# Latent attention: the rotary products of a head group moved ahead of its values, keys and queries, and the first group's opening written in another order

## The reference

```python
c_kv = rmsnorm(kv_a[..., :KV_LORA_RANK], ckv_norm)             # 128 wide, made earlier
k_nope = jnp.einsum('bsr,rhd->bshd', c_kv, w_uk)
v = jnp.einsum('bsr,rhd->bshd', c_kv, w_uv)
...
cq = rmsnorm(u @ w_dq, q_lora_norm)                            # 256 wide
q = jnp.einsum('bsr,rhd->bshd', cq, w_uq)
q_rope = apply_rope(q[..., QK_NOPE_DIM:], cos[None, :, None], sin[None, :, None])
...
s = (jnp.einsum('bqhd,bkhd->bhqk', qn_b, k_nope)
     + jnp.einsum('bqhr,bkr->bhqk', qr_b, k_rope))
p = jax.nn.softmax(s, axis=-1).astype(v.dtype)                 # causal, scaled
return jnp.einsum('bhqk,bkhd->bqhd', p, v)                     # 16 heads
```

## Time and profile before

| | |
|---|---|
| median of 3 runs | 1855.37 us (1854.82 to 1855.79) |
| the profiled execution | 1855.3 us, span of its instructions 1853.4 us |
| TensorE busy | 1823.8 us (98% of the span) |
| VectorE busy | 1568.9 us (85%) |
| ScalarE busy | 1148.2 us (62%) |
| GpSimd busy | 77.7 us (4%) |
| granted TensorE clock | 0.999 of full |

### The profile page before, as it was taken

How to read it: one execution, slowest core, us unless ns; L and a number is a source line. 1 busy time by engine, 2 the same in 40 slices (tenths; PEclk the granted TensorE clock), 3 DMA queues, 4 the chain that set the end, 5 groups by cost and what they waited for, 6 DMA issues and landing times.

```text
span 1853.4 us, 33830 instructions
## 1 busy us (share of the span) xinstructions
PE 1823.8 (98%) x13244; PEld 1702.7 (92%) x13244; DVE 1568.9 (85%) x1996; ACT 1148.2 (62%) x1478; POOL 77.7 (4%) x101
## 2 busy tenths in 40 slices
PE   8999999999999999999999999999999999999998
PEld 8999999999998889999999998899999998889997
DVE  7998899889886749997999799899889985879996
ACT  6665666666666637665666657666666656456664
POOL 1000100000000000000100000100010002010000
PEclk9999999999999999999999999999999999999999
DMA  7655465555553146555655443565545563345553
GB/s 273 216 196 200 164 217 196 190 182 204 204 196 144 48 149 215 205 204 182 216 204 198 145 146 117 194 242 203 202 169 207 199 214 122 119 149 183 207 195 107
DMA packets 61592, 339.18 MB, mean 183 GB/s; under 512 B 6976, under 2 KB 7360, under 8 KB 33088
## 3 DMA queue, kind: packets, MB, share of 16 engines
q1 hardware_dynamic: 59472, 330.00, 51.0%
q0 software_dynamic: 2032, 7.96, 1.2%
HBM read 336.89 MB, written 1.05 MB: 182 GB/s over the span
## 4 chain that ended last, share of the span: by engine, by line
PE 88%; DVE 7%; ACT 3%; issue 2%; DMA 1%; POOL 1%; DVEq 0%; SPq 0%; POOLq 0%; ACTq 0%
PE X L2051 60%; PE Y L2051 26%; DVE loA L1313 2%; DVE arena L1669 1%; DMA rawA<-in_wa 1%; ACT hiA L697 1%; DVE ol L1478 1%; PE X L2092 1%; ACT arena L1011 0%; DVE xs L1396 0%; DVE h L1403 0%; DVE arena L1834 0%; DVE arena L1771 0%; DVE xl L1353 0%; PE X L2075 0%
## 5 line engine op out<-in xcount | busy, mean ns | idle before, releaser
L2051 PE MATMUL X<-xh,hiA 128*128 128x256 f32 x2464 | 680.3, 278 | 6.0 <-DVE loA L1313 3.9
L2051 PE MATMUL X<-xl,hiA 128*128 128x256 f32 x2464 | 678.0, 277 | 0.0
L2051 PE MATMUL X<-xh,loA 128*128 128x256 f32 x2464 | 669.4, 277 | 0.0
L1313 DVE TENSOR_TENSOR loA<-rawA,hiA 128x2048 fp32r<-128x2048 f32 (+1 forms) x213 | 485.2, 2278 | 59.3 <-ACT hiA L697 59.0
L2051 PEld LDWEIGHTS X<-xh,hiA 128*128 128x128 f32 x2464 | 462.8, 188 | 8.9 <-DVE loA L1313 5.3
L2051 PEld LDWEIGHTS X<-xl,hiA 128*128 128x128 f32 x2464 | 463.4, 188 | 0.0
L2051 PEld LDWEIGHTS X<-xh,loA 128*128 128x128 f32 x2464 | 457.3, 188 | 0.0
L697 ACT ACTIVATE hiA<-rawA 128x2048 fp32r<-128x2048 f32 (+1 forms) x232 | 421.9, 1820 | 50.4 <-PE Y L2051 29.8
L852 ACT ACTIVATE act_sh<-X 128x512 f32<-128x512 f32 x168 | 100.7, 599 | 388.0 <-PE X L2051 388.0
L1524 DVE TENSOR_TENSOR sum_lo<-arena,sum_hi 128x2048 fp32r<-128x2048 f32 x72 | 164.5, 2285 | 1.5 <-ACT sum_hi L816 1.5
L816 ACT ACTIVATE sum_hi<-arena 128x2048 fp32r<-128x2048 f32 x72 | 137.2, 1905 | 0.0
(11 more groups left out here) (325 smaller groups left out, 3468.8 us busy)
## 6 DMA issues: line engine op xcount, KB each, us to landing
rawA<-in_wa SPq DMA_DIRECT2D x221, 1024.0 KB, 4.9
rawB<-in_wb SPq DMA_DIRECT2D x181, 512.0 KB, 4.1
row_gain<-in_rows POOLq DMA_DIRECT2D x8, 512.0 KB, 5.0
arena<-in_gla POOLq DMA_DIRECT2D x1, 1280.0 KB, 7.7
h<-in_x SPq DMA_DIRECT2D x2, 512.0 KB, 4.2
arena<-in_taps POOLq DMA_DIRECT2D x1, 576.0 KB, 4.9
arena<-in_pool POOLq DMA_DIRECT2D x1, 544.0 KB, 5.0
rawA<-in_wa SPq DMA_DIRECT2D x2, 256.0 KB, 6.4
```

Of the source, the lines that this page charges most:

```text
L1313: nc.vector.tensor_tensor(loA[p][:, cut], rawA[p][:, cut], hiA[p][:, cut].bitcast(f32), ALU.subtract).then_inc(a_lo, 1)
L2051: return say(nc.tensor.matmul(*args, **kw))
```

## The change

In groups 1 to 3 TensorE does the rotary products first, then the values, keys and queries. ScalarE copies each rotary bank into a new buffer `m_rope` in two extra copies per group, right behind the exponential of the same number, and that copy gives the bank back. VectorE turns from `m_rope` and tells so by a new semaphore `q_turned`, for which `scores` waits, and, for the buffer, the copy of two groups later. In group 0 the rotary products stay last and are turned out of the bank, but TensorE transposes the query latent before keys 0 and 1, starts the queries of heads 0 and 1 with the products of `cqh`, and does those of `cql` last; ScalarE copies the latent before `split_B(b + 1)` and does `split_A(a + 2)` behind the group's copies; VectorE puts `split_A(a + 2)` between the two turns and the second turn behind `maxima(0)`.

```diff
@@ -971,7 +973,7 @@
                 raw_squares(s, 1)
                 def values(g):
                     for t in range(TT):
-                        act.wait_ge(mproj_psum, 8 * g + 1 + t)
+                        act.wait_ge(mproj_psum, 8 * g + (3 if g else 1) + t)
                         nc.scalar.activation(m_v[:, g % 2, t, :], X[:, t, :], ACT.Copy
                                              ).then_inc(mproj_free[t], 1)
@@ -979,23 +981,28 @@
                     act.wait_ge(cq_psum, t + 1)
                     mean_square(s["norm_mid"] + t, Y[:, 2 + t, 0:2 * P], m_p[:, t, 0:2 * P], (2 * P) ** -0.5)
                 values(0)
-                split_B(b + 1, (b + 1) % 2)
                 for k in range(2):
                     act.wait_ge(cq_t, k + 1)
                     nc.scalar.activation(cqh[:, k, :], X[:, 2 + k, 0:TOKENS], ACT.Copy,
                                          scale=cols[:, COL["q_lora"] + k:COL["q_lora"] + k + 1]).then_inc(cq_hi, 1)
+                split_B(b + 1, (b + 1) % 2)
                 def projections(g, head=None):
                     n = a + 2 + g
                     if g:
+                        for p in range(2):
+                            exps(head, (p,))
+                            act.wait_ge(mproj_psum, 8 * g + 1 + p)
+                            if g > 1:
+                                act.wait_ge(q_turned, 2 * (g - 2) + p + 1)
+                            nc.scalar.activation(m_rope[:, p, :], X[:, p, 0:TOKENS], ACT.Copy
+                                                 ).then_inc(mproj_free[p], 1)
                         values(g)
                     for i in range(GROUP):
-                        if g and i < 2:
-                            exps(head, (i,))
                         if g == 1 and i >= 2:
                             split_A(n, n % 2, i - 2)
-                        act.wait_ge(mproj_psum, 8 * g + i + 3)
+                        act.wait_ge(mproj_psum, 8 * g + (5 if g else 3) + i)
                         nc.scalar.activation(m_qk[:, g % 2, i, :], X[:, i % 2 if g else i, :], ACT.Copy
                                              ).then_inc(mproj_free[i % 2], 1)
                     if g == 1:
...
@@ -1022,8 +1029,8 @@
                     act.wait_ge(mo_psum, i + 1)
                     nc.scalar.activation(oh(i), o_bank(i), ACT.Copy).then_inc(mo_hi, 1)
+                projections(0)
                 split_A(a + 2, a % 2)
-                projections(0)
                 for i in range(HEADS):
                     if i >= 2:
                         out_hi(i - 2)
...
@@ -1663,12 +1670,17 @@
             def turn_queries(g, p):
+                if g:
+                    dve.wait_ge(mproj_free[p], 4 * g + 1)
+                else:
+                    dve.wait_ge(mproj_psum, 7 + p)
                 for j in range(2):
                     rows = slice(64 * j, 64 * j + 64)
+                    straight = m_rope[rows, p, :] if g else X[rows, p, 0:TOKENS]
                     for part in range(2):
                         ins = nc.vector.tensor_tensor(m_qr[64 * part:64 * part + 64, g % 2, 2 * p + j, :],
-                                                      X[rows, p, 0:TOKENS], trig[rows, part, :], ALU.mult)
-                ins.then_inc(mproj_free[p], 1)
+                                                      straight, trig[rows, part, :], ALU.mult)
+                ins.then_inc(q_turned if g else mproj_free[p], 1)
             def latent(s):
                 norm_in(s)
...
@@ -1751,7 +1763,6 @@
                     elif g:
                         ahead(g)
                     for p in range(2):
-                        dve.wait_ge(mproj_psum, 8 * g + 7 + p)
                         turn_queries(g, p)
                 def maxima(i):
...
@@ -1776,10 +1787,13 @@
                     nc.vector.tensor_tensor(ol(i), o_bank(i), oh(i).bitcast(f32),
                                             ALU.subtract).then_inc(mo_lo, 1)
-                ahead(0)
-                projections(0)
+                split_B(b + 1, (b + 1) % 2)
+                turn_queries(0, 0)
+                split_A(a + 2, a % 2)
                 for i in range(HEADS):
                     maxima(i)
+                    if i == 0:
+                        turn_queries(0, 1)
                     if i >= 2:
                         out_lo(i - 2)
                     normalise(i)
...
@@ -2493,7 +2507,7 @@
                     m = b + g
                     pe.wait_ge(b_lo, m + 1)
                     for t in range(TT):
-                        bank(g, t)
+                        bank(g, 2 + t if g else t)
                         ins = by_tokens(X[:, t, :], ckvh[:, P * t:P * t + P], ckvl[:, P * t:P * t + P],
                                         hiB[m % 2][:, 512:1024], loB[m % 2][:, 512:1024], True, True)
                         ins.then_inc(mproj_psum, 1)
...
@@ -2533,8 +2547,6 @@
                 def projections(g):
                     n, m = a + 1 + g, b + g
-                    if g:
-                        values(g)
                     nh = hiA[n % 2][:, 0:1024].rearrange("p (h k c) -> p h k c", h=4, k=2)
                     nl = loA[n % 2][:, 0:1024].rearrange("p (h k c) -> p h k c", h=4, k=2)
                     rh = hiA[n % 2][:, 1024:1536].rearrange("p (h k c) -> p h k c", h=2, k=2)
...
@@ -2546,7 +2558,7 @@
                     def keys(i):
                         if g or i < 2:
-                            bank(g, 2 + i)
+                            bank(g, 4 + i if g else 2 + i)
                         by_latent(head_bank(i)[:, TOKENS:512], uh[:, P * i:P * i + P], ul[:, P * i:P * i + P],
                                   ckvh[:, :], ckvl[:, :], True, True)
...
@@ -2556,29 +2568,44 @@
                                             cql[:, k, :], k == 0, k == 1)
                         ins.then_inc(mproj_psum, 1)
+                    def rotary():
+
+                        wait_A(n)
+                        for p in range(2):
+                            bank(g, p if g else 6 + p)
+                            for k in range(2):
+                                ins = by_latent(X[:, p, 0:TOKENS], rh[:, p, k, :], rl[:, p, k, :], cqh[:, k, :],
+                                                cql[:, k, :], k == 0, k == 1)
+                            ins.then_inc(mproj_psum, 1)
+
                     if g == 0:
-                        for i in (2, 3, 0, 1):
-                            keys(i)
+                        keys(2)
+                        keys(3)
                         pe.wait_ge(cqs_done, 2)
                         query_latent()
-                        pe.wait_ge(cq_lo, 2)
+                        keys(0)
+                        keys(1)
                         pe.wait_ge(a_hi, n + 1)
                         pe.wait_ge(nope_lo, 1)
-                        for i in range(GROUP):
-                            queries(i)
+                        for k in range(2):
+                            pe.wait_ge(cq_hi, k + 1)
+                            for i in range(2):
+                                mm(X[:, i, 0:TOKENS], nh[:, i, k, :], cqh[:, k, :], start=k == 0, stop=False)
+                                mm(X[:, i, 0:TOKENS], nl[:, i, k, :], cqh[:, k, :], start=False, stop=False)
+                        pe.wait_ge(cq_lo, 2)
+                        for i in range(2):
+                            for k in range(2):
+                                ins = mm(X[:, i, 0:TOKENS], nh[:, i, k, :], cql[:, k, :], start=False, stop=k == 1)
+                            ins.then_inc(mproj_psum, 1)
+                        queries(2)
+                        queries(3)
+                        rotary()
                     else:
+                        rotary()
+                        values(g)
                         for i in range(GROUP):
                             keys(i)
-                            if i == 0:
-                                wait_A(n)
                             queries(i)
-                    wait_A(n)
-                    for p in range(2):
-                        bank(g, 6 + p)
-                        for k in range(2):
-                            ins = by_latent(X[:, p, 0:TOKENS], rh[:, p, k, :], rl[:, p, k, :], cqh[:, k, :], cql[:, k, :],
-                                            k == 0, k == 1)
-                        ins.then_inc(mproj_psum, 1)
                     owed.extend((a_free, b_free))
                 def scores(i):
...
@@ -2587,9 +2614,11 @@
                     if j == 0:
                         pe.wait_ge(mproj_free[0], 4 * g + 4)
                     if j == 1:
-                        pe.wait_ge(mproj_free[1], 4 * g + (2 if g else 3))
+                        pe.wait_ge(mproj_free[1], 4 * g + 3)
                     if j == 2:
                         pe.wait_ge(mproj_free[1], 4 * g + 4)
+                    if g and j % 2 == 0:
+                        pe.wait_ge(q_turned, 2 * (g - 1) + j // 2 + 1)
```

2 lines of the change are left out of this document (added).

## The result

The changed kernel takes 1858.23 us (median of 21 runs, 1857.0 to 1859.86) against 1855.29 us before (21 runs, 1854.62 to 1857.53): 2.94 us more. The ratio is 1.0016, with a 95% interval of 1.001 to 1.0022, so no change within 0.2%, though the interval lies above 1. The span of the profiled execution is 1856.9 us. ScalarE has six instructions more, the copies of the rotary banks (1484 in place of 1478), and TensorE as many matmuls as before.

The account below looks back on a forecast made before the run. TensorE is busy 98% of the span, so only its waits inside attention can change. Terms 2.17 - 0.59 - 0.33 = 1.25 us slower than the 1855.37 us median give 1856.6 us; range 1853.2 to 1859.3 us.

Parts of the forecast that it names:

- The upper end of the terms: Bounds of all terms together, -2.6 to +3.2 us; 3.2 lost if ScalarE's pieces in group 1 come 1 us later still.
- the low half's wait: Group 0: TensorE's wait of 1.26 us before the first query product, for the latent's low half, would be gone.
- new waits for the new copy: Groups 1, 2, 3: TensorE idle 1.4, 0.7 and 0.4 us before the first value product, released by the rotary copy.
- three signs of being wrong: Head 1's exponential well ahead of 591.4, ScalarE's second piece ending before 597.5, or a granted clock dip at 604 us.
- 2.17 us later than before: Group 1: `transpose_p(2)` at 606.57 in place of 604.40, VectorE's split and turns standing behind ScalarE's second piece.
- the opening: Group 0's new order: rotary products, first turn and scores of head 0 come 1.46 us earlier, between 1.2 and 1.53.
- Gain 0.59 us: Group 2: exponentials of head 6 start at 621.16 in place of 621.75 us.
- Gain 0.33 us: Group 3: `transpose_p(10)` comes at 641.33 in place of 641.66 us.
- the rival on the clock: Idle 2.8 us ahead of `transpose_p(2)` halves TensorE's clock: 1862.1 us, or 1859.3 if one head; chance 0.07.
- The turns' source: VectorE's turns from `m_rope` cost like turns from the bank; the skill's 0.065 us less each was not followed.
- The turns leave the path everywhere: Rival: all five TensorE waits shown in attention go, 5.75 us, 1849.6 us; chance 0.06.
- A part of it: Rival: group 1 even or keeps 0.80 us because ScalarE's pieces catch up, 1853.6 to 1854.4 us; chance 0.10.

Follow-up runs that it names:

- e3: Changed kernel with VectorE's two turns in group 1 put ahead of the split that waits for ScalarE: 1854.15 us, -0.46 against before.
- e4: Changed kernel with ScalarE's two pieces of the weight split in group 1 moved one head forward: 1855.91 us, +1.10 against before; repeated on another chip, 1856.05 us.
- third profile: Changed kernel run again unaltered, as control beside other kernels on one chip: 1857.29 us, +2.52 against before.
- e5: Changed kernel with both rotary copies ahead of both exponentials on ScalarE: 1856.03 us, +1.26 against before.
- e8: Changed kernel with eleven unused identity transposes on TensorE between the rotary products and the values of group 1: 1856.52 us, +1.75 against before.
- e10: Changed kernel with filler transposes in group 1, eleven ahead of the values and twenty ahead of `transpose_p(2)`: 1857.23 us, +2.20 against before.
- e6: Changed kernel with rotary copies ahead of the exponentials and, in group 1, turns ahead of the split: 1852.72 us, -2.05 against before.
- e7: Changed kernel with copies before exponentials, group 1 turns before the split, ScalarE's pieces one head earlier, `split_B` behind `copy_pt(0)`: 1851.98 us, -2.83 against before.
- e2: Changed kernel with group 0 in the old order, so only the rotary products moved ahead and copied out: 1857.49 us, +2.88 against before.

## Why the prediction was right

**Verdict and mechanism.** Forecast 1856.6 us, measured 1858.23, inside the range and within 0.2%. That is a shift of 2.94 us where 1.25 was forecast, so it is the path that was right, and the size only roughly. The upper end of the terms, +3.2, stood for ScalarE's pieces coming 1 us later; they came 0.34 us later, and 1.0 of the 1.7 us missing is in none of the terms (below). The steps came as written: the low half's wait gone, 1.23 us before the scores of head 0 (forecast about 1.3), new waits for the new copy of 1.53, 0.65 and 0.30 us (1.4, 0.7, 0.4), `transpose_p(2)` held for 2.62 us (about 2.8) by a split that waits for hiA, `weigh(0)` held for 0.65 (0.85), and no wait left before `transpose_p(6)` and `transpose_p(10)` (less than 0.7). None of the three signs of being wrong came: in the clock of before, the exponential of head 1 starts at 591.65 us, ScalarE's second piece ends at 599.07, and the granted clock of the profile is full from 592 to 650 us. Experiments e3 and e4 show the link on which the sum turned, by breaking it and by moving it.

**The sum was too small**, 1.25 us against 1.95 in the profile after. Three of its terms were off:

- "**2.17 us later than before**" measured 2.48. Of the 0.31, 0.11 is the opening (1.35 gained, not 1.46) and 0.13 is VectorE between the maxima of head 0 and those of head 1: they begin 14.20 us behind the first value product, where 13.96 was worked out. Another 0.1 is the handover from the new copy (593.63 + 0.37) to the value product at 594.14, for which I had allowed 0.05. From there the delay is constant: ScalarE's second piece ends, VectorE's split begins and the transposes come each 0.31 to 0.34 later than worked out.
- "**Gain 0.59 us**" in group 2 measured 0.32. The wait of 1.17 went and one of 0.65 came, which would leave 0.52; most of the rest went where I had priced nothing: the matmuls of the heads are 0.118 us apart in this group (618.08 to 621.26 for 27) where the group before took 0.113, 1.06 us a head and not 1.02. In the third profile they take 1.02 again, and the gain is 0.47.
- "**Gain 0.33 us**" in group 3 measured 0.21 (0.23 in the third profile).

**The remaining 0.6 to 1.0 us** of the median may lie in part in the rival on the clock. I had given it 0.07, put it ahead of `transpose_p(2)` only and priced it at 2.7 or 5.45 us, from the work of one or two heads at half rate. The traces of the changed kernel show it smaller (1.37 us), at another place (the head of group 1, behind the 1.52 us wait), and in only some executions. At the place that I had named it was seen once, in e5, where the stretch from `transpose_p(2)` to `transpose_p(3)` took 4.13 us in place of 3.07, and the count above points there too. The error was to argue that the clock "stayed full through waits of up to 1.50 us": one execution does not bound what another one does, and the new waits stand at other places than the old. Of the executions of the changed kernel, 28 of 43 have a mean clock of 0.998 or less, of those of the kernel before beside the last two of its three sets one of 66. A thousandth of the clock is, by my estimate from the span of 1856 us, about 1.9 us. The Trainium skill, "TensorE: Matmul & The Clock Gate", section "Why this matters for your kernels", warns of idle gaps in mid-kernel; I had written that no stage of the trace showed it. Its row is for longer gaps than any measured here, so the falls seen behind 1.52 and 2.62 us go beyond it. How much of the 0.6 to 1.0 us the clock makes is open: e8 came 0.77 us lower, but e10, without one low mean clock, kept 0.37 of it.

**The turns' source.** The Trainium skill, "VectorE: DVE Perf Modes", section on the TRN2 errata, would have made eight turns 0.5 us shorter out of `m_rope` than out of the bank. They take 3.46 to 3.47 us in place of 3.49: 0.003 us each, not 0.065. In one and the same profile there is no difference at all: four turns out of the bank take 1.72 or 1.73 us (group 0 of the changed kernel), and eight out of `m_rope` 3.46. The measurement decides, and going by the rows was right.

**The rivals.** "The turns leave the path everywhere" did not happen, for the reason given against it; e3, e6 and e7 show that it takes more than one reordered line to come near it, and that all the edits of e7 together are worth 2.8 of the 5.75 us listed, since waits of 1.23, 0.42, 0.66 and 0.43 us are left in groups 0 and 1. "A part of it" did not happen either: ScalarE's pieces did not catch up, they ended later than worked out.

## What to carry to other kernels

Freeing a bank early pays only where the instruction that uses the freed time is not itself queued behind something late: before moving work off a path, read on the engine that does it what stands ahead of it in its list, and whether that waits for a third engine. Here a weight split that was not needed before group 2 stood ahead of the turns, and putting the turns first turned +2.6 us into -0.5, and with the copy ahead of the exponentials into -2.05. A new copy has to be placed by what it waits behind, not only by its length: 0.38 us of work made a wait of 1.5 us.

## What was not expected of the hardware

**The clock can fall behind waits of 1.5 to 2.6 us, and does so in some executions only.** In the changed kernel's profile it fell at 26 us, in code that the change does not touch, behind a wait of 1.82 us for a split. That wait is in each of the 13 profiles read, between 1.20 and 1.82 us long, and this is the longest; behind the 1.76 us of e6 the clock stayed full. The rows of the changed kernel's profile:

```profile
25.24 0.39 PE L2065 MATMUL X<-xh,hiA 128*128 128x256 f32 x1 [1.82 <-DVE loA L1320]
...
26.88 0.42 PE L2065 MATMUL X<-xh,hiA 128*128 128x256 f32 x1
27.09 0.42 PE L2065 MATMUL X<-xl,hiA 128*128 128x256 f32 x1
```

```profile
22.00:26.00 4.00, 2.18 (x19) 1.98 (x18) 2.96 (x3) 1.88 (x4) 0.00 (x0) 1.00 0.42 135
26.00:30.00 4.00, 4.00 (x23) 4.00 (x23) 3.48 (x8) 3.04 (x4) 1.08 (x2) 0.57 0.92 286
30.00:34.00 4.00, 4.00 (x30) 3.77 (x29) 1.97 (x1) 1.29 (x2) 0.00 (x0) 1.00 0.98 376
```

The matmuls go from 0.114 to 0.214 us apart more than a microsecond after TensorE had started again. The clock lost in these windows (0.43 of 4 us) is about the 1.62 us by which attention begins later in that profile. It is not the change's doing: in the two other profiles of the changed kernel attention begins at 576.22 and 576.13 us. In e5 it was 0.84 and 0.73 of full in the windows around and behind the wait of 2.62 us, which ends at 606.04:

```profile
604.00:608.00 4.00, 1.96 (x10) 1.79 (x11) 2.88 (x11) 3.28 (x10) 0.00 (x0) 0.84 0.04 14
608.00:612.00 4.00, 4.00 (x21) 3.54 (x20) 2.44 (x8) 2.41 (x10) 0.00 (x0) 0.73 0.00 0
```

In the five other profiles with the same wait of 2.62 us (the three of the changed kernel, e2 and e8) it stayed full behind it. So a single profile shows whether a wait cost clock once, not whether it does. The mean clock over many executions tells more, and a page that shows 9 in every slice hides such a fall altogether: 3 us are less than a tenth of a slice.
